# Normalization between the stages of a six-layer block stack: worked in place on the accumulator and transpose banks, with the order of the work around it redone

## What is computed

```python
for i in range(4):                        # layer norm behind each half
    x = layer_norm(DN_ALPHA * x + mixer(x), ln_g[i, 0], ln_b[i, 0])
    x = layer_norm(DN_ALPHA * x + swiglu(x), ln_g[i, 1], ln_b[i, 1])
for l in range(2):                        # rms norm ahead of each half
    x = x + mixer_2(rmsnorm(x, attn_norm_g[l]))
    x = x + ffn(rmsnorm(x, ffn_norm_g[l]))
```

## Time and profile before

| | |
|---|---|
| median of three runs | 2586.67 us |
| profiled execution, its own time | 2585.18 us |
| its span, first to last instruction | 2583.4 us |
| mean granted TensorE clock | 0.969 |
| PE busy | 2454.9 us, 95% |
| VectorE busy | 1477.3 us, 57% |
| ScalarE busy | 1324.3 us, 51% |
| GpSimd busy | 480.9 us, 19% |
| HBM read | 395.51 MB, 154 GB/s |

### The profile page before, as it was taken

One profiled execution on the slowest core, in us unless ns is written; L12 is line 12 of the kernel. 1 busy time (PEld: TensorE's weight loads), 2 busy tenths in 40 slices (PEclk: granted clock), 3 DMA queues, 4 the chain that ended last, 5 costly groups with the idle time before them and its releaser, 6 DMA issues.

```text
span 2583.4 us, 36889 instructions
## 1 busy us (share of the span) xinstructions
PE 2454.9 (95%) x15388; PEld 2162.7 (84%) x15388; DVE 1477.3 (57%) x2114; ACT 1324.3 (51%) x1974; POOL 480.9 (19%) x370
## 2 busy tenths in 40 slices
PE   7999999999899998999989989999999999899999
PEld 5689977777699776998769979889899898798898
DVE  5455454544654545555555456656676666566766
ACT  4454455554544555544445446546565565465654
POOL 3230041322400223101410001342100004421000
PEclk9799999999899999999889999999999989999999
DMA  6145543333355433554315544334445443344453
GB/s 243 49 176 183 184 158 114 115 115 130 114 194 182 164 132 132 193 186 175 132 66 196 183 160 156 126 143 147 166 176 182 179 155 123 132 156 169 165 194 131
DMA packets 58182, 398.94 MB, mean 154 GB/s; under 512 B 6816, under 2 KB 7072, under 8 KB 11680
## 3 DMA queue, kind: packets, MB, share of 16 engines
q1 hardware_dynamic: 56864, 393.75, 41.9%
q10 hardware_dynamic: 1152, 2.83, 0.3%
HBM read 395.51 MB, written 1.05 MB: 154 GB/s over the span
## 4 chain that ended last, share of the span: by engine, by line
PE 82%; DVE 8%; ACT 5%; issue 3%; POOL 1%; DMA 0%; SPq 0%; DVEq 0%; ACTq 0%; POOLq 0%
PE b L1139 12%; PE b L1141 12%; PE b L1140 12%; PE b L1073 12%; PE b L1074 11%; PE b L1075 11%; PE b L1078 8%; PE b L1082 4%; DVE wlo L1780 2%; ACT whi L1415 2%; DVE xl L1792 1%; ACT full L1411 1%; DVE st L1843 1%; DVE xn L1841 1%; DVE xn L1854 0%
## 5 line engine op out<-in xcount | busy, mean ns | idle before, releaser
L1780 DVE TENSOR_TENSOR wlo<-raw,whi 128x2048 fp32r<-128x2048 f32 x351 | 823.0, 2348 | 441.6 <-ACT whi L1415 441.4
L1415 ACT ACTIVATE whi<-raw 128x2048 fp32r<-128x2048 f32 x362 | 690.8, 1910 | 356.4 <-PE b L1141 225.6
L1139 PE MATMUL b<-xh,whi 128*128 128x256 f32 x2560 | 728.7, 285 | 0.0
L1141 PE MATMUL b<-xh,wlo 128*128 128x256 f32 x2560 | 722.8, 282 | 0.0
L1140 PE MATMUL b<-xl,whi 128*128 128x256 f32 x2560 | 722.8, 282 | 0.0
L1139 PEld LDWEIGHTS b<-xh,whi 128*128 128x128 f32 x2560 | 486.5, 190 | 8.1 <-issue 6.1
L1140 PEld LDWEIGHTS b<-xl,whi 128*128 128x128 f32 x2560 | 486.7, 190 | 1.9
L1141 PEld LDWEIGHTS b<-xh,wlo 128*128 128x128 f32 x2560 | 486.2, 190 | 0.0
L1073 PE MATMUL b<-whi,xh 128*128 128x512 f32 x832 | 356.0, 428 | 54.4 <-issue 38.0
L1074 PE MATMUL b<-wlo,xh 128*128 128x512 f32 x832 | 337.3, 405 | 0.0
L1075 PE MATMUL b<-whi,xl 128*128 128x512 f32 x832 | 336.8, 405 | 0.0
(11 more groups left out here) (225 smaller groups left out, 2896.3 us busy)
## 6 DMA issues: line engine op xcount, KB each, us to landing
raw<-in_w SPq DMA_DIRECT2D x362, 1024.0 KB, 4.8
gt<-in_rows SPq DMA_DIRECT2D x8, 512.0 KB, 3.9
bt<-in_rows SPq DMA_DIRECT2D x8, 512.0 KB, 4.8
abq<-in_rows ACTq DMA_DIRECT2D x2, 768.0 KB, 4.7
x<-in_x SPq DMA_DIRECT2D x1, 1024.0 KB, 6.3
bc<-in_rows SPq DMA_DIRECT2D x4, 256.0 KB, 5.0
out<-x SPq DMA_DIRECT2D x4, 256.0 KB, 2.1
msk<-in_masks SPq DMA_DIRECT2D x1, 768.0 KB, 7.8
```

The source lines that it names most:

```text
L1139: pe.matmul(out, wh[:, k, cs], ah[:, kk, :], start=kk == 0 and s == 0, stop=False, skip_group_check=True)
L1141: last = pe.matmul(out, wl[:, k, cs], ah[:, kk, :], start=False, stop=final and k == 3, skip_group_check=True)
L1415: return ac.activation(out, i, ACT.Copy)
L1780: ve.tensor_tensor(B.wlo[s][:, :], B.raw[r][:, :], B.whi[s][:, :], ALU.subtract).then_inc(sem["loV"], 1)
```

## The change

`add` writes its sum back into the accumulator bank and takes the statistics there; `norm` reads the bank and writes `xn`, and frees the bank. Gain and bias of the transposed parts are applied by VectorE in the transpose bank, in place; ScalarE copies the high part from the bank, and VectorE subtracts it from the bank, which frees it. `full` is no longer used here, and GpSimd makes no `xl` any more. In the order: each `closed(t, c)` issues one pending low part ahead of its `add`; at boundary 7 `parts(0)` stands behind `norm`, `affine` and `rms` of t = 1; `parts(1)` is issued inside the stretch (1,0) of the next projection, after 18 matmuls, with both its `parts` ahead of both low parts; `let_go` of the tail tile moves to its last `close`; and no `wlo` is issued by `pump` while `late` is not empty.

```diff
     def pump(self, n=1):
-        if self.lows:
+        if self.lows and not self.late:
             self.lowtick += 1
...
+                if first and half == 1 and t == k == 0:
+                    while self.late:
+                        self.late.pop(0)()
                 yield
             if t:
                 self.let_go(held[half])
-            if first and half == t == 0:
-                while self.late:
-                    self.late.pop(0)()
...
                 if t and c:
                     self.gone_by_bank(held[-1], ("acc", a, 1, 1))
+                    self.let_go(held[-1])
                 closed(t, c)
...
-        def parts(t, put_off):
+        def parts(t):
             for q in range(2):
                 self.bank(("turned", a + 1, t, q), 4 + 2 * t + q)
+                self.counts("xf", (a + 1, t, q))
+                self.counts("xhi", (a + 1, t, q))
                 self.step("parts", a + 1, t, q)
-                self.counts("xhi", (a + 1, t, q))
-                if put_off:
-                    later.append((t, q))
-                else:
-                    low(t, q)
...
+                later.append((t, q))
+
+        def low():
+            if later:
+                self.step("xlo", a + 1, *later.pop(0))
...
         def closed(t, c):
-            if a < 7 and c and t and later:
-                low(*later.pop(0))
+            low()
             self.step("add", a, t, c)
...
-            if a == 7 and t:
-                parts(0, True)
-                while later:
-                    low(*later.pop(0), "G")
-            if later:
-                low(*later.pop(0))
...
                 self.step("rms", a, t)
+            if a == 7 and t:
+                parts(0)
+
+        def second():
+            parts(1)
+            while later:
+                low()
...
             if a < 11:
-                self.late.append(lambda: (parts(1, False), self.let_go(self.tail)))
+                self.late.append(second)
...
@@ ScalarE norm
-        act(y[:, 512:1024], y[:, 512:1024], ACT.Identity, scale=s[:, 16:17],
-            bias=s[:, 15:16]).then_inc(sem["xna"], 1)
+        act(B.xn[:, t, 512:1024], B.bank[b][:, :], ACT.Identity, scale=s[:, 16:17],
+            bias=s[:, 15:16]).then_inc(sem[f"empty{b}"], 1)
...
@@ ScalarE parts
-        for k in range(4):
-            kk = 4 * q + k
-            last = act(f[:, 128 * k:128 * k + 128], bk[:, 128 * k:128 * k + 128], ACT.Identity, scale=g[:, kk:kk + 1],
-                       bias=0.0 if bias is None else bias[:, kk:kk + 1])
-        last.then_inc(sem[f"empty{b}"], 1)
-        a.wait_ge(f"empty{b}", n + 1)
+        a.wait_ge("xf", mark["xf", (x, t, q)])
         copy(B.xh[:, 4 * q:4 * q + 4, 128 * t:128 * t + 128],
-             f.rearrange("p (k n) -> p k n", k=4)).then_inc(sem["xhi"], 1)
+             B.bank[b][:, :].rearrange("p (k n) -> p k n", k=4)).then_inc(sem["xhi"], 1)
...
@@ VectorE 
+    def parts(x, t, q):
...
+        v.wait_ge(f"full{b}", n + 1)
+        for k in range(4):
+            kk, cs = 4 * q + k, slice(128 * k, 128 * k + 128)
+            if bias is None:
+                last = ve.tensor_scalar(bk[:, cs], bk[:, cs], g[:, kk:kk + 1], None, ALU.mult)
+            else:
+                last = ve.tensor_scalar(bk[:, cs], bk[:, cs], g[:, kk:kk + 1], bias[:, kk:kk + 1], ALU.mult, ALU.add)
+        last.then_inc(sem["xf"], 1)
+
     def xlo(x, t, q):
...
-        ve.tensor_tensor(B.xl[:, 4 * q:4 * q + 4, sl], B.full[:, q, :].rearrange("p (k n) -> p k n", k=4),
-                         B.xh[:, 4 * q:4 * q + 4, sl], ALU.subtract).then_inc(sem["xloV"], 1)
+        ve.tensor_tensor(B.xl[:, 4 * q:4 * q + 4, sl], B.bank[b][:, :].rearrange("p (k n) -> p k n", k=4),
+                         B.xh[:, 4 * q:4 * q + 4, sl], ALU.subtract).then_inc(sem[f"empty{b}"], 1)
...
@@ VectorE add
-        y = B.xn[:, t, h]
-        ve.tensor_tensor(y, B.bank[b][:, :], B.x[:, t, h], ALU.add).then_inc(sem[f"empty{b}"], 1)
-        v.wait_ge(f"empty{b}", n + 1)
-        B.stat_i = v.mine(ve.bn_stats(B.st[:, t, 6 * c:6 * c + 6], y))
+        i = v.mine(ve.tensor_tensor(B.bank[b][:, :], B.bank[b][:, :], B.x[:, t, h], ALU.add))
+        v.wait_ge("own_v", i)
+        B.stat_i = v.mine(ve.bn_stats(B.st[:, t, 6 * c:6 * c + 6], B.bank[b][:, :]))
...
@@ VectorE norm
-        ve.tensor_scalar(y[:, 0:512], y[:, 0:512], s[:, 16:17], s[:, 15:16], ALU.mult,
-                         ALU.add).then_inc(sem["xnv"], 1)
+        ve.tensor_scalar(B.xn[:, t, 0:512], B.bank[b][:, :], s[:, 16:17], s[:, 15:16], ALU.mult,
+                         ALU.add).then_inc(sem[f"empty{b}"], 1)
```

More of the change, by code:

```diff
@@ L187, in __init__ @@
         self.units = 0
-        self.tail = None
     def step(self, *what):
@@ L1047, in low_sem, with normal_ready @@
     return "lo" + o.low_on[i]
-def part_sem(o, x, t, q):
-    return "xlo" + o.low_on["x", x, t, q]
+def normal_ready(lane, o, a, t, halves=(0, 1)):
+    for c in halves:
+        b, n = o.use["acc", a, t, c]
+        lane.wait_ge(f"empty{b}", n + 1)
 def mixer_of(u):
@@ L1062, in activation_ready @@
     def activation_ready(x, t, q):
[L1063 to L1067 removed]
+        b, n = use["turned", x, t, q]
+        p.wait_ge(f"empty{b}", n + 1)
     def weight_ready(w):
@@ L1191, in parts @@
         b, n = use["turned", x, t, q]
-        what = ("normal" if x < 8 else "scaled", x - 1, t)
-        if q == 0:
-            p.wait_ge("xnv", mark["xnv", what])
+        if x < 8:
+            normal_ready(p, o, x - 1, t, (q,))
+        elif q == 0:
+            p.wait_ge("xnv", mark["xnv", ("scaled", x - 1, t)])
         else:
-            p.wait_ge("xna", mark["xna", what])
+            p.wait_ge("xna", mark["xna", ("scaled", x - 1, t)])
         p.wait_ge(f"empty{b}", n)
@@ L1452, in norm @@
     def norm(a_, t):
-        s, y = B.st[:, t, :], B.xn[:, t, :]
+        s = B.st[:, t, :]
+        b, n = use["acc", a_, t, 1]
         a.wait_ge("stat_v", mark["stat_v", ("variance", a_, t)])
@@ L2283, in mparts @@
         ve.tensor_tensor(B.xl[:, sl, :], B.merged[:, sl, :], B.xh[:, sl, :], ALU.subtract).then_inc(sem["mlo"], 1)
-    does = {"begin": begin, "loV": lo, "turn_x": turn_x, "xloV": xlo, "angles": angles, "add": add, "norm": norm,
+    does = {"begin": begin, "loV": lo, "turn_x": turn_x, "parts": parts, "xlo": xlo, "angles": angles, "add": add, "norm": norm,
             "affine": affine, "rms": rms, "sinks": sinks, "kv_in": kv_in, "twice": twice, "q_bias": q_bias,
@@ L2481, in branch @@
             ge.tensor_tensor(out, out, B.sigs[d][:, 2 * j:2 * j + 2, :], ALU.add).then_inc(sem["mgg"], 1)
-    does = {"loG": lo, "xloG": xlo, "scale_x": scale_x, "scale_gb": scale_gb, "carry": carry, "rope": rope, "k2": k2,
+    does = {"loG": lo, "scale_x": scale_x, "scale_gb": scale_gb, "carry": carry, "rope": rope, "k2": k2,
             "merge": merge, "setup": setup, "xs": xs, "xde": xde, "off": off, "decay": decay, "gate_z": gate_z,
@@ L2657 @@
 SEMS = ["const", "cols", "pos", "x", "ab", "abo", "gb", "mask0", "mask1", "small", "gmg", "gmb", "ws", "out",
-        "own_v", "own_a", "own_g", "hi", "loV", "loG", "gone", "xhi", "xloV", "xloG", "xnv", "xna", "xg", "stat_v",
+        "own_v", "own_a", "own_g", "hi", "loV", "loG", "gone", "xf", "xhi", "xnv", "xna", "xg", "stat_v",
         "stat_a", "eps", "tables", "rope", "twice", "k2", "floor", "exp", "pv", "ohi", "merge_g", "merged", "silu",
```

46 lines of the change are left out of this document (13 added, 33 removed).

## The result

The changed kernel takes 2548.3 us (median of four, 2546.5 to 2550.2) against 2585.8 us of the kernel before on the same chip: a ratio of 0.9855, 95% interval 0.9838 to 0.9872. The profiled execution has a span of 2547.6 us, 35.8 less than before. I forecast 2550 us, and -36.7.

The account below looks back on a forecast made before the run. TensorE, busy 2454.9 of 2583.4 us, loses time in stands and low clock at layer boundaries. Boundaries 1 to 5 -23.2, 0 and 6 -8.0, 8 to 10 -11.1, boundary 7 +5.6: -36.7 us, so 2550 us, range 2536 to 2570.

Parts of the forecast that it names:

- The main chain: VectorE's small steps from T to F set F-T in boundaries 1 to 5: 13.20 us instead of 18.03, saving 23.2 us.
- The stand at F: TensorE's idle time ahead of F, the first matmul of `tok(half 0, t 1)` after a boundary; forecast 1.8 us.
- The normalization from the bank: VectorE's normalization reading a bank takes 0.74 us, instead of 0.55 alone or 1.60 beside GpSimd.
- T: Start of a boundary's first transposes on TensorE; forecast to come 0.19 us later.
- Boundaries 0 and 6: Clock already low before T is over, TensorE 0.6 us later than the chain; saved 4.0 us each, 8.0 us.
- Boundaries 8 to 10: No bias, `rms` unchanged: F-T 11.65 us instead of 15.37, saved 3.7 us three times, 11.1 us.
- F-T: Time from T to F at a boundary; forecast 13.20 us instead of 18.03 in boundaries 1 to 5.
- Boundary 7: `parts(0)` moves behind `rms(7,1)`: first `tok` 5.3 us late, F 5.6 us later, one wait of some 12 us.
- Rival 1: The clock falls in the new stands, 1.7 us each, 12 us in seven boundaries: 2562 us; chance 0.2, whole or part.
- Rival 2: VectorE's bank write has its own price: slower from 0.43 us a piece, 2606 us at 0.55; chance 0.07.
- Rival 3: GpSimd still stretches bank normalization (0.74 to 2.1 us) and bank pieces: 2569 us; chance 0.1, shared with pieces of 0.41.
- Rival 4: Larger gain: pieces 0.25 us apart throughout and the clock never low, 2538 us; chance 0.11.

Follow-up runs that it names:

- experiments 1 and 2: The runs act_in_bank (2540.4 us) and pieces_to_sbuf (2610.0 us), in that order.
- experiment 10: The kernel before, with GpSimd making each `wlo` tile in four operations of 512 columns instead of one of 2048; 2562.6 us, ratio to before 0.9908.
- experiment 4: The changed kernel with the first half's pieces and low parts at boundary 7 ahead of `norm(7,1)` again; 2541.0 us, ratio to before 0.9828.
- pieces_twice: Experiment 6: the changed kernel with each bank's four gain-and-bias pieces done twice, the second set waiting for the first; 2631.0 us (one run).
- pieces_to_sbuf: The changed kernel, VectorE's pieces in the new order but written to `full` in SBUF, high and low parts taken from there; 2610.0 us (one run).
- share: The changed kernel with boundary 7's first-half pieces ahead of `norm(7,1)` and two of each half's eight pieces on ScalarE; 2536.9 us, ratio to before 0.9809.
- act_in_bank: The kernel before, ScalarE's pieces written to the bank, high and low parts read there, VectorE also making boundary 7's low parts; 2540.4 us, ratio 0.9829.
- late12: The changed kernel with the second transposes back after 12 matmuls of the next stage instead of 18; 2548.6 us (one run).
- both: The changed kernel with boundary 7's first-half pieces ahead of `norm(7,1)`, and q0's low part ahead of q1's pieces; 2540.8 us, ratio to before 0.983.
- split: `both` with the first half's q1 pieces of boundaries 0 to 6 on ScalarE, adds ahead of low parts, second transposes after 12 matmuls; 2541.3 us, ratio 0.9827.

## Why the prediction was right

**The main chain** (13.20 for boundaries 1 to 5) measured 13.12. Its terms: eight pieces with bias 2.64, measured 2.56 and 2.55 from the first piece to the start of the low part (the 2.66 and 2.65 of the rows hold the end of the last piece, which overlaps it); without bias 2.16, measured 2.07 (1843.50 to 1845.57 below); low part 0.68, measured 0.69; low part start to add start 0.61, measured 0.60; add to add 1.32 + 0.61, measured 1.94; second add to normalization 2.46, measured 2.47; normalization to transposes 0.80, measured 0.87. The stand at F was forecast as 1.8 and is 1.50, the one before the second transposes 0.8 and is 0.61. The saving from the stretched low part, read from two rows of one operation, is what experiments 1 and 2 showed to be the whole gain. My reading of those rows as a stretch was loose: it is a wait for GpSimd's operation to end (experiment 10), which for the sum made no difference, because the bank avoids either.

```profile
1843.50 2.17 DVE L1783 TENSOR_SCALAR b<-b,col 128x128 f32<-128x128 f32 x8 [0.75 <-PE b L1075]
1845.57 0.68 DVE L1792 TENSOR_TENSOR xl<-b,xh 128x512 fp32r<-128x512 f32 x1
```

**The normalization from the bank** was mis-sized: forecast 0.74, measured 0.81. I added the price of a second scalar in SBUF (0.06) to the 0.68 of the `add`, an operation of another kind with no scalar at all. No run prices a single scalar on 512 columns from a bank. The two rows that I set beside the Trainium skill's "Why PSUM operands drop a tier" (0.49 and 0.68) differ in the same way; the pair that fits is this normalization itself, 0.55 from SBUF and 0.81 from the bank, and it agrees in sign. T comes 0.3 us later instead of 0.19, seven times a tenth of a microsecond; the normalization explains 0.07 of that tenth.

**Boundaries 0 and 6** gained 4.6 us where I had 4.2 before T's delay (18.02 to 13.41 and 18.03 to 13.41). **Boundaries 8 to 10**: F-T 11.69 to 11.70, forecast 11.65.

**Boundary 7** was forecast at a loss of 5.6 us, with a wait of some 12; it lost 6.6, with a wait of 12.9. Counted from T, the first projection is 5.9 us later than before, where I had 5.3. Two terms were too good: VectorE's wait for ScalarE's root fell from 2.74 us to 0.36 and not to nothing, and the 0.3 us from less stretching did not come, since `affine`'s products take 2.58 + 0.69 us where they took 1.63 + 1.65. The way from there to F is 0.66 us longer (9.32 to 9.98), where I had 0.3. The order there costs 7.8 us in all, as experiment 4 measures; before the change those steps stood in the better order.

**Rival 1** (a lower clock at F) did not come: in the three microseconds behind F the granted clock is 1.00 in all eleven boundaries, with stands of at most 1.5 us ahead. Where the stand at F was longer, it fell: to 0.62 behind 4.31 us in `pieces_twice`, to 0.50 behind 2.99 us in boundary 3 of `pieces_to_sbuf`. **Rival 2** lacked its condition: pieces at 0.32 us apart, and a bank write as long as one to SBUF. **Rival 3** fell by the normalization of 0.81 beside GpSimd. **Rival 4** needed pieces 0.25 us apart, which only the ones without bias come near (0.26). By the Trainium skill's cycle table ("VectorE: DVE Perf Modes", "The TRN2 errata"), whose column is for results that go to SBUF, a piece is an estimated 0.26 us. The trace has that for the pieces without bias, and 0.06 more for the ones with bias.

**What I had taken at nothing and what the text did not have.** The ten stretches between F and the next T are longer by 3.0 us in sum. Five are longer by 0.27 to 0.31 each, which is the later T (1.5 us). The other five differ by -1.3, +1.0, +0.1, +4.8 and -3.0. The two large ones are the mixers of the last two layers, where the matmuls are the same in both kernels. The windows of the narrow matmuls of the first of these, before and after (columns as in the window of experiment 6):

```profile
1601.00:1611.00 10.00, 10.00 (x76) 10.00 (x76) 3.96 (x12) 2.31 (x5) 0.00 (x0) 0.83 0.00 0
...
1574.70:1584.70 10.00, 10.00 (x58) 10.00 (x58) 1.77 (x11) 1.74 (x3) 0.00 (x0) 0.61 0.00 0
```

TensorE is busy throughout in both, at a granted 0.83 and 0.61. The stretch from F of boundary 7 to T of 8, beside the granted clock of the window from 41 to 53 us behind F and of the one from 155 to 165:

| kernel | stretch, us | clock at +41 | clock at +155 |
|---|---|---|---|
| before | 303.90 | 0.86 | 1.00 |
| share | 303.99 | 0.86 | 1.00 |
| act_in_bank | 305.54 | 0.72 | 1.00 |
| late12 | 305.47 | 0.72 | 1.00 |
| both | 307.27 | 0.72 | 0.83 |
| changed | 308.68 | 0.57 | 0.86 |

A step of the clock is 1.4 to 1.8 us. In the stretch from F of 9 to T of 10 it was the kernel before that had 0.57 and 0.85 and took 308.65, against 305.63 of the changed one, so the two nearly cancel (+4.8, -3.0). Which kernel has which clock follows none of my edits; what decides it stays open. That the total comes within 0.9 us of the forecast is therefore in part luck. Part by part, forecast and measured: F-T of 0 to 6 -32.5 and -33.7, boundary 7 +5.6 and +6.6, 8 to 10 -11.1 and -11.4, the stretches in between +1.3 (the later T) and +3.0, the ends nothing and -0.3. The clock of these stretches also sets how fine a span may be read here: a difference of 2 to 3 us between single profiles of two kernels is nothing.

## What to carry to other kernels

Look for one operation that has two durations in a trace, and for what ran beside the long one. Here a subtraction with two SBUF inputs waited for GpSimd's operation to end (0.69 us became 3.10); keeping the intermediate in its PSUM bank cured it, with no other engine and no other order needed, and shorter GpSimd operations cured half of it. A chain cut at one end must also release what stands behind it (`both` and `split` shortened F by 0.5 to 1.1 us and gained nothing, since the next weight tile came later or the matmuls in between were late), and in a change of several parts each order should be timed by itself: the one of boundary 7 cost 7 of the 45 us that the place of an operand had given.

## What the runs showed of the hardware

- VectorE reads a PSUM bank and writes it in place at the price of a write to SBUF: eight 128-column pieces 2.66 against 2.64 us.
- A second per-partition scalar costs VectorE 0.06 us on a 128-column piece in a bank (0.32 against 0.26 us apart) and on 512 columns in SBUF. The normalization with two scalars on 512 columns takes 0.81 us from a bank and 0.55 from SBUF.
- An operation of VectorE with two SBUF inputs of 512 columns (0.69 us alone) that starts during a GpSimd operation with two inputs ends 0.54 to 0.56 us after it; one of 2048 columns (2.29 us alone) that has to wait ends 2.15 us after it. It waits, and is not slowed. The normalization with a single SBUF input (0.55 us alone) ends 0.27 to 0.29 us after it: 1.65 us beside `carry`. With a bank as input none of these operations was stretched: the low part's mean over its 44 instances in the changed kernel is 682 ns.
- The granted clock of one and the same busy stretch of narrow matmuls came out at 0.57, 0.72 or 0.86 in different kernels, in steps of 1.4 to 1.8 us.
